# A third width, 144 columns, for the gate and up products of experts with 129 to 144 rows

## The chip, the core and the metric

The kernel runs on one core of a Trainium2 chip. The metric is the device time of one execution in microseconds; a lower number is better. The kernel before takes 750.63 us, the median of three runs.

## What is computed

One layer of an encoder over 768 tokens of width 1024. After a mixing part (projection, a recurrent group, a spatial gating group, an output projection) comes the part that the change touches, a mixture of 16 experts. A router picks two experts for each token, and each expert is a gated product with an inner width of 512:

```python
for e in range(N_EXPERTS):
    hdn = jax.nn.silu(t @ w1[e]) * (t @ w3[e])      # gate and up
    out = out + gate[:, e:e + 1] * (hdn @ w2[e])    # down
```

The reference does this for all tokens; `gate` is zero for the tokens that did not choose expert e. A per-layer embedding part and a last norm follow. All of it is float32.

## The kernel before, in words

**Rounds.** The expert part is a chain of 16 rounds, one for each expert, r = 0 to 15. A round works on the rows of the tokens that chose its expert, gathered ahead by GpSimd into `moe["xg", par]` (the first 128 rows) and `moe["xg2", par]` (up to 32 more, `CAP` is 160). `par` is r modulo 2; even rounds read the transposed rows from `regT`, odd ones from `regN`, so these names in the trace tell the two apart. Rows over 160 would go to further rounds at the end; the register `more` counts these.

**One round on TensorE** (`one_round`, L990): it reads the number of rows of its expert and of the next one from `table` into registers (L992, L994). Then come two halves. Each half computes two of the four blocks of 128 inner columns, gate and up, with `hidden` (L955): two blocks times two weights times 8 steps over the width of 1024, 32 float32 matmuls, whose moving operand has `n` columns, one for each row of the expert. Behind the first half stand four transposes of the next expert's rows (L933), behind the second half four more. Then the down products, 24 matmuls in two parts (L964 to L966), between which the further 32 rows of the next expert are turned if it has over 128 (L935), and at last, if the round's own expert has over 128 rows, 16 matmuls for those further rows (L973, L976).

**The width.** The 32 matmuls of a half are in the program once for each width of `CLASSES` (L52), and `by_size` (L979) puts them behind branches on the register: it splits the list of widths in two, asks whether the count fits the lower part, and goes down until one width is left. With the two widths 128 and 160 that is one branch ahead of each half, and a jump over the 160 body for those that ran the 128 body. The seven pairs of rounds from 2 to 15 are one loop, `pe.Fori(1, NE // 2)` at L1064, whose body is an even and an odd round; rounds 0 and 1 are written out ahead of it (L1062, L1063). Behind the loop stands a branch over the code for rows above 160 (L1068), then the products of the embedding part (L875).

**Others.** ScalarE (silu, copies) and VectorE (products with up, the low parts of numbers) read from PSUM at the full 160 columns in every round, whatever the width was (L1289, L1783). SyncE loads three weights of 2 MB for each round into slots of `ring`, each as soon as TensorE has done with what lay there (L507, L510).

Of the kernel before, what the change touches and what calls it, by code (L numbers as in the profile page):

```python
# [48 lines left out]
MAX_OVER = 2 * NTOK // CAP  # L49
NROUND = NE + MAX_OVER  # L50
NSLOT = NROUND * CAP
CLASSES = (128, 160)  # L52
NYG = 4
MASKED = -3.0e38

# [5 lines left out]
def hybrid_encoder_kernel(nc, x_prompt, x_sample, p_prompt, p_sample, g_mix, w_in, conv_w, conv_b, lru_w_a,  # L61
# [11 lines left out]
    with ExitStack() as ctx:  # L73
# [277 lines left out]
        class Chain:  # L351
# [5 lines left out]
            def post(self, ins):  # L357

                self.n += 1
                ins.then_inc(self.sem, 1)  # L360
# [350 lines left out]
        def _(pe):  # L711
# [266 lines left out]

            def by_size(count, body, sizes=CLASSES):  # L979

                if len(sizes) == 1:
                    body(sizes[0])
                    return
                low = sizes[:len(sizes) // 2]
                with pe.If(count < low[-1] + 1):
                    by_size(count, body, low)
                with pe.Else():
                    by_size(count, body, sizes[len(low):])
# [456 lines left out]
        def _(dve):  # L1445
# [275 lines left out]
            for b in range(4):  # L1721
                post(V.memset(bank[b][:, :].rearrange("p (f s) -> p f s", f=2)[:, :, CLASSES[0]:CAP], 0.0))
            post(V.memset(bank[5][0:CAP2, 4 * NE:], 0.0))
# [211 lines left out]
```

## Time and profile before

| what | us |
|---|---|
| median of 3 runs (750.43 to 753.56) | 750.63 |
| the profiled execution | 751.04 |
| its span, first to last instruction | 749.3 |
| TensorE busy with matmuls | 722.1 |
| mean granted TensorE clock | 0.992 of full |
| rounds 0 to 15 (first gate product to last down product) | 288.5 to 652.9 |

The profile tells one execution. PE are the matmuls and PEld the weight loads of TensorE; a row on PEldq is TensorE's sequencer, which reads the program, takes the branches and hands the matmuls on. A float32 matmul of the program gives two PE and two PEld records, so a half of a round shows as 64 matmuls.

### The profile page before, as it was taken

To read this page: it belongs to the slowest core of one execution; us is meant where nothing else is said; L and a number is where in the kernel's file an instruction comes from. 1 tells how busy PE (TensorE), PEld (TensorE's weight loads), DVE (VectorE), ACT (ScalarE), POOL (GpSimd) and SP (SyncE) were. 2 spreads that over 40 slices of the span, in tenths; PEclk is the share of its full clock that TensorE was granted. 3 is DMA by queue.
4 is the path that set the end of the run, shared out by engine and by line. 5 is a ranking of instruction groups with operands and counts; after the bars stand their busy time and mean duration, and the time that the engine had idled before them with its cause. 6 is when DMAs were issued, how large, how long until landed. Compare 5 with 4: busy or idle time off the path is not lost.

```text
span 749.3 us, 12071 instructions
## 1 busy us (share of the span) xinstructions
PE 722.1 (96%) x4424; PEld 624.1 (83%) x4425; DVE 420.6 (56%) x729; ACT 323.3 (43%) x593; POOL 136.8 (18%) x170
## 2 busy tenths in 40 slices
PE   6999999999999988999999999999999999899996
PEld 4987777787888857989988988999999999848885
DVE  5867986894654488424442342445455444567664
ACT  6508659673502135324441332344344433484243
POOL 5465104151001003000000000000000000043420
PEclk9999999999999999999999999999999999999998
DMA  9909924402225177978996595799999999363212
GB/s 312 285 1 328 270 55 154 169 1 105 92 88 193 57 280 247 313 270 307 367 360 242 215 363 200 288 338 343 364 346 337 330 336 361 139 205 113 98 43 85
DMA packets 78162, 168.59 MB, mean 225 GB/s; under 512 B 7581, under 2 KB 19305, under 8 KB 78122
## 3 DMA queue, kind: packets, MB, share of 16 engines
q1 hardware_dynamic: 70128, 141.53, 53.5%
q0 software_dynamic: 4448, 14.62, 6.3%
q10 hardware_dynamic: 3546, 11.91, 4.1%
q8 instruction: 26, 0.43, 0.2%
q14 instruction: 14, 0.11, 0.0%
HBM read 143.99 MB, written 24.05 MB: 224 GB/s over the span
## 4 chain that ended last, share of the span: by engine, by line
PE 92%; DVE 3%; ACT 2%; issue 1%; POOL 0%; ACTq 0%; DMA 0%; POOLq 0%; DVEq 0%
PE bank L743 35%; PE bank L955 32%; PE bank L731 5%; PE bank L964 4%; PE bank L966 4%; PE bank L965 4%; PE bank L723 2%; PE bank L933 2%; ACT ring_r L1377 1%; PE bank L976 1%; PE bank L973 1%; PE bank L875 1%; PE bank L715 1%; DVE regN L1458 0%; PE bank L935 0%
## 5 line engine op out<-in xcount | busy, mean ns | idle before, releaser
L743 PE MATMUL bank<-ring_r,regT_r 128*128 128x512 f32 (+1 forms) x648 | 161.5, 384 | 3.3 <-DVE regT_r L1571 1.7
L743 PEld LDWEIGHTS bank<-ring_r,regT_r 128*128 128x128 f32 x648 | 117.9, 188 | 28.7 <-issue 3.4
L955 PE MATMUL bank<-regT,ring 128*128 128x128 f32 (+1 forms) x1024 | 123.7, 282 | 2.9 <-issue 1.9
L955 PEld LDWEIGHTS bank<-regT,ring 128*128 128x128 f32 x1024 | 121.7, 191 | 5.3 <-issue 5.1
L955 PE MATMUL bank<-regN,ring 128*128 128x128 f32 (+1 forms) x1024 | 123.2, 281 | 0.1
L955 PEld LDWEIGHTS bank<-regN,ring 128*128 128x128 f32 x1024 | 122.1, 191 | 1.1 <-issue 0.5
L643 POOL DMA_INDIRECT regT<-n_scratch,idsi x17 | 16.1, 950 | 307.8 <-PEq L922 178.2
L743 PE MATMUL bank<-regT_r,ring_r 128*128 128x256 f32 (+1 forms) x256 | 66.1, 347 | 1.8 <-POOL ring_r L608 1.8
L1783 DVE TENSOR_TENSOR regR<-regR,bank 128x256 f32<-128x256 f32 x32 | 13.5, 421 | 89.2 <-ACT regR L1289 88.9
L1289 ACT ACTIVATE regR<-bank 128x320 f32<-128x320 f32 x32 | 13.8, 431 | 92.6 <-PE bank L955 92.6
L743 PEld LDWEIGHTS bank<-regT_r,ring_r 128*128 128x128 f32 x256 | 46.2, 199 | 7.2 <-DVE h_r L1464 2.0
L1132 ACT ACTIVATE regN<-h 128x1024 f32<-128x1024 f32 x23 | 24.3, 1061 | 60.9 <-DVE h L1592 40.8
L965 PE MATMUL bank<-ring_r,regR_r 128*128 128x512 f32 x128 | 49.9, 390 | 0.0
L438 POOL TENSOR_TENSOR ring_r<-ring,ring_r 128x1024 fp32r<-128x1024 f32 x16 | 41.4, 2621 | 27.3 <-ACT ring_r L430 27.3
L743 PE MATMUL bank<-h_r,ring_r 128*128 128x512 f32 (+1 forms) x128 | 44.3, 346 | 0.0
L596 POOL TENSOR_SCALAR small<-small 128x1 f32<-128x1 f32 (+1 forms) x26 | 10.1, 389 | 167.3 <-ACT regN L1132 100.7
L1795 DVE TENSOR_TENSOR ring_r<-ring,wsT_r 128x512 fp32r<-128x512 f32 x32 | 20.7, 688 | 29.8 <-ACT wsT_r L1304 29.8
L743 PE MATMUL bank<-ring_r,h_r 128*128 128x512 f32 x96 | 37.4, 389 | 0.0
L1801 DVE COPY regN<-bank 128x512 f32<-128x512 f32 x16 | 11.1, 691 | 45.8 <-PE bank L966 45.8
L1304 ACT ACTIVATE wsT_r<-ring 128x512 fp32r<-128x512 f32 x32 | 18.4, 622 | 33.1 <-issue 24.8
L1311 ACT ACTIVATE regN<-bank 128x512 f32<-128x512 f32 x16 | 9.6, 597 | 48.5 <-PE bank L966 48.5
L743 PE MATMUL bank<-ring_r 128*128 128x512 f32 x96 | 30.3, 396 | 0.0
(319 smaller groups left out, 1240.0 us busy)
## 6 DMA issues: line engine op xcount, KB each, us to landing
ring<-in_w_exp_down SPq DMA_DIRECT2D x16, 2048.0 KB, 15.9
ring<-in_w_exp_gate SPq DMA_DIRECT2D x16, 2048.0 KB, 9.4
ring<-in_w_exp_up SPq DMA_DIRECT2D x16, 2048.0 KB, 16.6
ring<-in_w_in SPq DMA_DIRECT2D x3, 2048.0 KB, 11.7
y_scratch<-zeros SPq DMA_DIRECT2D x4, 1408.0 KB, 12.9
y_scratch<-regN ACTq DMA_DIRECT2D x11, 384.0 KB
h<-in_x_sample SPq DMA_DIRECT2D x8, 512.0 KB, 10.0
y_scratch<-zeros SPq DMA_DIRECT2D x4, 1024.0 KB, 11.0
```

The lines of the kernel that those rows point to most:

```text
L438: engine.tensor_tensor(ringR[:, lo, c], ring[:, lo, c], ringR[:, hi, c].bitcast(F32), ALU.subtract).then_inc(lo_ready[unit], 1)
L643: nc.gpsimd.indirect_dma_start(moe["xg", par][0:n, :], None, n2_dram, bass.IndirectOffsetOnAxis(ap=ids[0:n, :], axis=0)).then_inc(gathered ...
L723: q = nc.tensor.transpose(ps(name)[:src.shape[1], at:at + n], src, ident[0:n, 0:n])
L731: q = nc.tensor.matmul(out, a, b, start=(k == 0), stop=(k == len(pairs) - 1))
L743: q = nc.tensor.matmul(out, a, b, start=(n == 0), stop=(n == len(passes) - 1))
L955: q = nc.tensor.matmul(bank[b][:, col:col + n], slot3(s)[:, k, f * P:(f + 1) * P], moe["xT", par][:, k, 0:n], start=(k == 0), stop=(k == K ...
L964: nc.tensor.matmul(out[:, :], x_high, high, start=(f == 0), stop=False)
L965: nc.tensor.matmul(out[:, :], x_high, low, start=False, stop=False)
L966: q = nc.tensor.matmul(out[:, :], x_low, high, start=False, stop=(f == F4 - 1))
L1132: nc.scalar.activation(ntok[:, i, :], h[:, i, :], ACT.Square, accum_out=dst).then_inc(done, 1)
L1304: nc.scalar.activation(down_hi[f][j], down_part(par, f, j), ACT.Copy).then_inc(down_high_done, 1)
L1795: V.tensor_tensor(down_low(par, f, j), down_part(par, f, j), down_hi[f][j].bitcast(F32), ALU.subtract).then_inc(down_low_done, 1)
```

## The change

`CLASSES` gets a third width. For each half `by_size` now writes three bodies: for at most 128 rows as before, for 129 to 144 rows one of 144 columns, for more one of 160. The list is split into (128) and (144, 160), so a second branch stands ahead of the two wider bodies, and none is added on the way to the 128 body.

```diff
-CLASSES = (128, 160)
+CLASSES = (128, 144, 160)
```

What that adds to TensorE's program, on the piece of the difference for the first half of round 0, the first of ten such places (two halves in each of rounds 0 and 1, of the two rounds of the loop, and of the round for rows above 160):

```order
@@ -649,4 +649,7 @@
 L955 MATMUL bank<-regT,ring 128x128 x32
 L985 UNCONDITIONAL_BRANCH
+L985 COMPARE_AND_BRANCH
+L955 MATMUL bank<-regT,ring 128x144 x32
+L985 UNCONDITIONAL_BRANCH
 L955 MATMUL bank<-regT,ring 128x160 x32
 L987 UNCONDITIONAL_BRANCH
```

The 144 body stands between the other two, with a branch ahead of it and a jump behind it. The other engines' programs are the same as before.

The head of the loop and the first half of its even round, on TensorE, before:

```order
L1064 ISA
L992 TENSOR_LOAD table
L992 ISA x2
L994 ISA
L994 TENSOR_LOAD table
L994 ISA x2
L997 ISA
L998 ISA
L1002 ISA
L985 COMPARE_AND_BRANCH
L955 MATMUL bank<-regT,ring 128x128 x32
L985 UNCONDITIONAL_BRANCH
```

and the same place from the branch on in the changed program:

```order
L985 COMPARE_AND_BRANCH
L955 MATMUL bank<-regT,ring 128x128 x32
L985 UNCONDITIONAL_BRANCH
L985 COMPARE_AND_BRANCH
L955 MATMUL bank<-regT,ring 128x144 x32
L985 UNCONDITIONAL_BRANCH
L955 MATMUL bank<-regT,ring 128x160 x32
L987 UNCONDITIONAL_BRANCH
```

The loop holds four such places, so its body is longer by 4 times 32 matmuls and their branches. A round with at most 128 rows now jumps over two bodies where it jumped over one.

## Rows read from the trace of the kernel before

**Rows 1.** The page: TensorE's busy time, and the chain that ended last by line.

```profile
PE 722.1 (96%) x4424; PEld 624.1 (83%) x4425; DVE 420.6 (56%) x729; ACT 323.3 (43%) x593; POOL 136.8 (18%) x170
...
PE bank L743 35%; PE bank L955 32%; PE bank L731 5%; PE bank L964 4%; PE bank L966 4%; PE bank L965 4%; PE bank L723 2%; PE bank L933 2%; ACT ring_r L1377 1%; PE bank L976 1%; PE bank L973 1%; PE bank L875 1%; PE bank L715 1%; DVE regN L1458 0%; PE bank L935 0%
```

**Rows 2.** Waits of TensorE, 285 to 660 us: total us, times, longest.

```profile
PE bank L955 <- issue: 1.9, 5, 0.9
```

**Rows 3.** Waits of SyncE's queue, 240 to 660 us, same columns.

```profile
SPq L510 <- PE bank L955: 211.5, 14, 18.2
```

**Rows 4.** Groups by line and shape: busy us, mean ns, idle before.

```profile
L955 PE MATMUL bank<-regN,ring 128*128 128x160 f32 x256 | 35.5, 299 | 0.1
L955 PE MATMUL bank<-regT,ring 128*128 128x160 f32 x256 | 35.5, 299 | 0.9 <-issue 0.9
```

**Rows 5.** Timeline of PE, rounds 0 and 1: start, us, line, tiles, count.

```profile
296.18 7.31 PE L955 MATMUL bank<-regT,ring 128*128 128x128 f32 x64
303.33 0.60 PE L933 MATMUL bank<-ident,regT 128*128 128x128 f32 x4
...
309.88 0.39 PE L966 MATMUL bank<-regR_r 128*128 128x512 f32 x1
310.33 8.96 PE L955 MATMUL bank<-regN,ring 128*128 128x160 f32 x64
...
319.57 8.86 PE L955 MATMUL bank<-regN,ring 128*128 128x160 f32 x64
328.26 0.60 PE L933 MATMUL bank<-ident,regT 128*128 128x128 f32 x4
```

**Rows 6.** Timeline of PE where the loop turns, rounds 3 to 4 and 7 to 8.

```profile
379.73 0.39 PE L966 MATMUL bank<-regR_r 128*128 128x512 f32 x1
381.05 8.96 PE L955 MATMUL bank<-regT,ring 128*128 128x160 f32 x64 [0.93 <-issue]
...
486.16 7.40 PE L955 MATMUL bank<-regT,ring 128*128 128x128 f32 x64 [0.25 <-issue]
```

**Rows 7.** Branches of `by_size`, whole run: ns min/median/max, first and last start.

```profile
L985 PEldq COMPARE_BRANCH  x56: 67/169/436, 288.4 to 644.9; - x56
```

**Rows 8.** The same line, 309 to 311 us and then 435 to 437 us.

```profile
L985 PEldq COMPARE_BRANCH  x1: 322/322/322, 310.0 to 310.0; - x1
...
L985 PEldq COMPARE_BRANCH  x1: 212/212/212, 435.9 to 435.9; - x1
```

**Rows 9.** Timeline of PE where the loop turns behind round 5.

```profile
437.44 0.39 PE L973 MATMUL bank<-regR_r 128*64 128x512 f32 x1
437.67 0.57 PE L955 MATMUL bank<-regT,ring 128*128 128x160 f32 x3
```

**Rows 10.** The loop's closing branch, whole run.

```profile
L1064 PEldq COMPARE_BRANCH  x7: 67/209/218, 378.5 to 650.8; - x7
```

**Rows 11.** Instruction packets by DMA queue, whole run: packets, MB, share.

```profile
q8 instruction: 26, 0.43, 0.2%
```

**Rows 12.** The same queue from 0 to 337 us.

```profile
q8 instruction: 16, 0.26, 0.3%
```

**Rows 13.** The same queue from 337 to 376 us.

```profile
q8 instruction: 5, 0.08, 0.9%
```

**Rows 14.** The same queue from 652 to 750 us.

```profile
q8 instruction: 5, 0.08, 0.3%
```

**Rows 15.** The branch over the code for rows above 160.

```profile
L1068 PEldq COMPARE_BRANCH  x1: 3317/3317/3317, 651.5 to 651.5; - x1
```

**Rows 16.** Timeline of PE behind the loop.

```profile
652.51 0.39 PE L966 MATMUL bank<-regR_r 128*128 128x512 f32 x1
655.02 12.26 PE L875 MATMUL bank<-ring,regX 128*128 128x512 f32 x24 [2.12 <-issue]
```

**Rows 17.** Busy time by stretch: PE, PEld, DVE, ACT, POOL, PEclk, DMA, GB/s.

```profile
655.00:657.70 2.70, 2.68 (x4) 1.31 (x5) 0.68 (x1) 0.00 (x0) 0.00 (x0) 0.58 0.44 124
278.00:285.00 7.00, 6.17 (x32) 2.75 (x32) 6.09 (x33) 0.79 (x2) 3.23 (x3) 0.76 0.59 202
```

**Rows 18.** Timeline of PE: eight matmuls of L875 at full clock, then across a dip.

```profile
270.32 3.67 PE L875 MATMUL bank<-ring,regX 128*128 128x512 f32 x8 [0.79 <-issue]
...
279.37 5.40 PE L875 MATMUL bank<-ring,regX 128*128 128x512 f32 x8
```

## The prediction

> **What bounds the kernel now.** I read the page first [rows 1]: TensorE is busy for 722 of 749 us, and the chain that ended last runs through its matmuls, 32% of the span through line 955, the products that the change narrows. Next the waits inside the expert part [rows 2]: ahead of line 955 TensorE stands still for 1.9 us in all 16 rounds, and for nothing but its own issue. SyncE's queue is the one that waits, 211.5 us for TensorE to give a slot of weights back [rows 3], so the weights come early. A microsecond less, or more, on TensorE between 288 and 653 us is therefore a microsecond of the end. The third thing to read is how TensorE gets its program, which the change makes longer: branches and instruction packets [rows 7 to 16].
>
> **Which rounds change.** The trace has 256 records of 160 columns on regN and as many on regT [rows 4]; a round has 128, so two odd and two even rounds have over 128 rows. By their places they are rounds 1, 4, 5 and 6. How many rows each has no view tells; worked out from the reference's inputs, experts 1, 4, 5 and 6 get 136, 133, 153 and 146. Rounds 1 and 4 take the new width, 5 and 6 stay at 160.
>
> **What the narrower products save.** From the start of a half's first product to the start of the transposes behind it a half takes 303.33 - 296.18 = 7.15 us at 128 columns and 328.26 - 319.57 = 8.69 us at 160 [rows 5]. Half way between them are 7.92 us, a saving of 0.77 us a half and, for four halves, 3.1 us. If time went purely by columns a half would be 8.69 x 144/160 = 7.82 us and the saving 3.5 us; if it moved in steps of 32 columns the saving would be nothing. I take 3.1, since 7.15 to 8.69 is already nearly the ratio of the columns. ScalarE and VectorE read 160 columns as before, and wait for TensorE, so they lose nothing.
>
> **What the branches cost.** A branch of by_size takes 67 to 436 ns, 169 in the median [rows 7]. In half 1 it is hidden: the five waits on issue [rows 2] all stand ahead of a half 0, and a second branch is hidden there too, under products and transposes still queued. In half 0 of round 1 the branch of 322 ns [rows 8] ends in the 0.22 us by which the first product comes late (310.33 against 309.88 + 0.23) [rows 5], and round 4 starts 0.93 us late [rows 6]. One more branch is paid at these two places, 0.1 us each: 0.2 us.
>
> **What the longer program costs.** This is the large term. In straight code instruction packets of 16 KB come all the way, 16 of them up to 337 us [rows 12]. While the loop is gone through for the first time, 337 to 376 us, there are 5 more [rows 13]. Behind it there are 5 [rows 14], and the whole run has 26 [rows 11]: 16 + 5 + 5. So in the 276 us in which the loop turns six more times, not one packet is fetched; TensorE keeps the whole loop. Counted from the order of the program, with four instructions for a float32 matmul, the loop has about 1,350 instructions of a program of about 7,150. With 26 packets for that program a packet holds some 270, and the loop is 5 packets long. It covers parts of six, and the one ahead of the last is fetched too: at least seven are kept. The change adds four bodies of 128 instructions and their branches, some 530. The loop then is about 1,880 long, 7 packets, covers parts of eight or nine, and with the one ahead nine or ten must be kept.
>
> The trace has the price of such a branch once. The one at line 1068 jumps over code that was never fetched and takes 3.3 us [rows 15], while a closing branch of the loop takes 0.21 us [rows 10]: 3.1 us more. Behind line 1068 TensorE has run dry for 2.12 us [rows 16], with a few products queued as cover. At the loop's turns there is less cover. It turns six times:
>
> - Behind rounds 3, 7, 9, 11 and 13, whose successor already starts 0.25 to 0.93 us late [rows 6], nothing is left to hide under: 5 x 3.1 = 15.5 us.
> - Behind round 5 the branch of the next round is done at 436.1 us [rows 8] and the queue holds work until 437.67 [rows 9], so 1.5 us are hidden and 1.6 us are paid.
> - The clock: twice TensorE stood still for about 2.1 us, ahead of 278.6 and of 655.02, and twice the granted clock then fell, to 0.76 and 0.58 in the mean of these stretches [rows 17], that is partly to the lower of its two levels, 1.2 GHz. Eight matmuls of line 875 took 5.40 us across such a dip and 3.67 us without [rows 18], 1.7 us more. After gaps of 3.3 us and more I expect it at each of the five turns, 8.5 us; bounds 0 and 8.5.
> - The first pass: rounds of at most 128 rows jump over 260 instructions at once, about a packet, where only one is fetched ahead. This may stall between 0 and 8 us over rounds 0 to 3; the five packets of 39 us [rows 13] become seven. I take 1.
>
> **The sum.** Against the profiled execution: 751.0 - 3.1 + 0.2 + 15.5 + 1.6 + 8.5 + 1 = 774.7 us. That execution lies 0.4 us above the median of 750.63, so the forecast is 774.3 us. This case's own range is 765 (no dip of the clock) to 781 (each fetch a microsecond longer, since in the loop it shares the DMA engines with the weights).
>
> **A rule on the other side of the rows.** The closing branch jumps back over five packets in 0.21 us, and no packet follows it [rows 10 to 14]. The same section of the Trainium skill also says that a taken branch whose target lies outside a window of two pages fetches that page. If this held for TensorE, the loop before would already pay at every turn, the misses would stand in both kernels, and the sum would be 751.0 - 3.1 + 0.2 - 0.4 = 747.7 us in place of 774.3. The rows contradict it, and I give it no chance.
>
> **The rivals.**
>
> - *The loop still fits.* TensorE keeps nine or more packets, and only the saving is left: 751.0 - 3.1 + 0.2 - 0.4 = 747.7 us, with the bounds of the saving 747 to 750.8. For it: the loop turns six times without one fetch. Against it: nothing seen has needed more than seven. This is the case on the other side, slightly faster; it decides at the size of the store, at or above the loop's span plus one.
> - *It fits, but the first pass stalls.* Up to 8 us on rounds 0 to 3 from jumps that run past the packet fetched ahead: 750 to 756 us. For it: the jumps get twice as long while fetches stay one ahead. Against: before, no round of the first pass is longer than the later ones of its width.
> - *The loop is fetched anew at each turn.* If a miss at the head discards what is kept, all packets come again in each of six passes, and the jumps over 260 instructions run past them: 1 to 4 us more in each of seven passes, or 780 to 800 us. For it: line 1068 shows that a jump outside what is kept restarts the fetching, with two packets within 5 us behind 652. Against: products queued ahead cover part of each stall, at line 1068 about 1.2 us (3.3 less the 2.12 run dry).
> - *The change does nothing here.* If no expert had 129 to 144 rows, only length would be added. The counts of 133 and 136 are far from both ends, so I give it no share.
>
> **How the numbers follow.** Loop head missed at each turn: 0.45, my forecast. Fetched anew with further stalls: 0.27. Still fits, saving alone: 0.20. Fits, with stalls in the first pass: 0.08. A difference of 0.5%, 3.75 us, is about what a measurement of this kernel can tell from no change. Faster than 746.9 us needs more than the largest saving, 0.03. Between 746.9 and 754.4 lie nearly all of "still fits" and half of the stalls in the first pass, 0.23. Slower than 754.4 us is the rest, 0.74. The range runs from 748, which takes in most of the case where the loop fits, to 795, which leaves out the end of the worst one.
>
> **What would show it.** Right if the profile after has: products of 144 columns in rounds 1 and 4, halves of about 7.9 us; far more than the 26 to 31 instruction packets that a longer program alone would need, at least one or two for each turn, between 380 and 660 us; closing branches at line 1064 of about 3 us in place of 0.21; idle time put down to issue ahead of each even round's first product; and dips of the clock behind it. One fetch of the head per turn means the forecast; seven or eight packets per turn mean the third rival. It is wrong if no instruction packet falls in the later passes of the loop and the closing branch still takes 0.2 us. Then the time must be near 748, and the store is larger than I took it to be.

## The result, and the profile after

The changed kernel takes 841.76 us in the median of four executions (825.98 to 854.03), the kernel before 750.53 us in the same sessions: 91 us more. The ratio is 1.105, with a 95% interval of 1.100 to 1.110; it is made from the two shorter executions, 825.98 and 835.67 us, while the profile below is of the longest, 854.03 us. The forecast of 774 us was right in its direction and in the part of the chip, and far off in size: 24 us slower were forecast, 91 were measured, and the range ended at 795.

The page of the profile after, against [rows 1] and [rows 11]:

```profile
span 852.3 us, 12083 instructions
PE 750.0 (88%) x4424; PEld 647.7 (76%) x4425; DVE 420.7 (49%) x729; ACT 324.4 (38%) x593; POOL 137.6 (16%) x170
PEclk9999999999999799999789899798897988999998
q8 instruction: 84, 1.38, 0.7%
PE 84%; issue 10%; DVE 3%; ACT 3%; ACTq 0%; POOL 0%; DMA 0%; POOLq 0%; DVEq 0%
```

The number of matmuls is the same and every other engine is as busy as before. Three things are new: 84 instruction packets where there were 26, 10% of the chain put down to issue, and a granted clock that falls again and again from the 14th of 40 slices on.

The waits of TensorE between 285 and 760 us (total, times, longest), against [rows 2]:

```profile
PE bank L955 <- issue: 57.3, 16, 9.0
PE bank L933 <- issue: 14.7, 7, 3.6
```

Before, these were 1.9 us and none. So 70 us are time in which TensorE had no instruction to run, either ahead of a half or ahead of the transposes behind it. The matmuls themselves take 750.0 - 722.1 = 27.9 us more, though fewer columns pass: that is the clock. Over the loop the mean granted clock (the column PEclk, the third from the right) is 0.91, where it was 1.00. After, then before:

```profile
345.00:752.00 407.00, 339.10 (x2307) 311.56 (x2305) 136.52 (x279) 122.78 (x265) 21.52 (x24) 0.91 0.68 244
...
337.60:652.90 315.30, 313.38 (x2314) 291.60 (x2312) 136.40 (x281) 121.78 (x265) 21.58 (x24) 1.00 0.85 310
```

70 + 28 and a wait ahead of line 944 that is 1.6 us longer than before make 100 of the 103 us between the two profiled executions.

The branches (count, ns min/median/max), against [rows 10], [rows 7] and [rows 15]:

```profile
L1064 PEldq COMPARE_BRANCH  x7: 67/6878/7333, 397.4 to 752.9; - x7
...
L985 PEldq COMPARE_BRANCH  x68: 68/234/6785, 288.6 to 746.3; - x68
...
L1068 PEldq COMPARE_BRANCH  x1: 3463/3463/3463, 753.8 to 753.8; - x1
```

The closing branch takes 6.1 to 7.3 us each time it is taken (the seventh time, 67 ns, the loop ends), not 0.2 and not the 3.3 I had. Its first start, 397.4 us, is 18.9 us later than before [rows 10]: that much is lost ahead of the first turn, and some 83 us in the six turns and the passes behind them. The jumps of by_size stall too, up to 6.8 us. And the packets by stretch, 0 to 345 us, 345 to 397 us (first pass of the loop), 397 to 753 us (six more passes), against [rows 12 to 14]:

```profile
q8 instruction: 18, 0.29, 0.3%
...
q8 instruction: 7, 0.11, 0.9%
...
q8 instruction: 54, 0.88, 1.0%
```

54 packets in six passes are nine a pass: the whole loop is fetched anew each time.

The narrower products do what they should. Round 4, second half, takes 427.12 - 419.28 = 7.84 us, where a half of 160 columns took 8.69 [rows 5]:

```profile
419.28 8.01 PE L955 MATMUL bank<-regT,ring 128*128 128x144 f32 x64
427.12 0.60 PE L933 MATMUL bank<-ident,regT 128*128 128x128 f32 x4
```

### The profile page after: what moved, and what is told of

The parts are those of the page before. It is cut to its first block, busy times and chain, and to the rows that moved or that the text cites. A ratio compares the mean times of both kernels' runs of the same rounds, so it can differ in the third digit from the quotient of the medians.

```text
span 852.3 us, 12083 instructions
## 1 busy us (share of the span) xinstructions
PE 750.0 (88%) x4424; PEld 647.7 (76%) x4425; DVE 420.7 (49%) x729; ACT 324.4 (38%) x593; POOL 137.6 (16%) x170
## 4 chain that ended last, share of the span: by engine, by line
PE 84%; issue 10%; DVE 3%; ACT 3%; ACTq 0%; POOL 0%; DMA 0%; POOLq 0%; DVEq 0%
PE bank L743 31%; PE bank L955 30%; PE bank L731 4%; PE bank L964 4%; PE bank L966 4%; PE bank L965 4%; PE bank L723 2%; PE bank L933 2%; ACT ring_r L1377 1%; PE bank L976 1%; PE bank L973 1%; PE bank L715 0%; PE bank L875 0%; DVE regN L1458 0%; PE bank L935 0%
## 5 line engine op out<-in xcount | busy, mean ns | idle before, releaser
L955 PE MATMUL bank<-regT,ring 128*128 128x128 f32 (+2 forms) x1024 | 142.5, 307 | 50.8 <-issue 48.8
L955 PEld LDWEIGHTS bank<-regT,ring 128*128 128x128 f32 x1024 | 139.3, 217 | 55.5 <-issue 55.3
L955 PE MATMUL bank<-regN,ring 128*128 128x128 f32 (+2 forms) x1024 | 126.9, 286 | 8.6 <-issue 8.6
L955 PEld LDWEIGHTS bank<-regN,ring 128*128 128x128 f32 x1024 | 124.7, 197 | 11.0 <-issue 10.8
L965 PE MATMUL bank<-ring_r,regR_r 128*128 128x512 f32 x128 | 51.9, 405 | 0.0
L933 PE MATMUL bank<-ident,regT 128*128 128x128 f32 x128 | 20.3, 284 | 14.7 <-issue 14.7
```

The source lines that it names most:

```text
L933: q = nc.tensor.transpose(bank[4][:, a * P:(a + 1) * P], moe["xg", par][:, k * P:(k + 1) * P], ident[:])
L955: q = nc.tensor.matmul(bank[b][:, col:col + n], slot3(s)[:, k, f * P:(f + 1) * P], moe["xT", par][:, k, 0:n], start=(k == 0), stop=(k == K ...
L965: nc.tensor.matmul(out[:, :], x_high, low, start=False, stop=False)
```

## The experiments

The instruction counts of the loop below are good to some 50 instructions; between two kernels they differ by some 130 for each body of a half. A packet is taken at 256 instructions: e8 has 32 bodies of some 130 more than e9 and fetches 17 packets more, some 245 to a packet. The times of the kernel before in these sessions had medians of 751.4 to 753.2 us; each ratio is against it.

### e1: the same length, no narrower product

```diff
-CLASSES = (128, 144, 160)
+CLASSES = (128, 160, 160)
```

> The widths are (128, 160, 160): as much code as in the change, but no product gets narrower; it does all of the reference's work. Theory A, the length of TensorE's program costs the time: as slow as the change and 3 us more, 830 to 860 us, some 84 instruction packets, closing branches of the loop of 6 to 7 us. Theory B, the 144-column products themselves do it (slower on TensorE, or something that reads them): 750 to 752 us.

Measured: 841.05 us, ratio 1.118 (1.114 to 1.123), 70 packets, closing branches of 6.4 us in the median. The loss is in the length of the program. The 144-column products have no part in it.

The 70 packets are unevenly spread. Two of the six passes behind the first fetch two packets, as my forecast had it for all of them, the other four nine. The passes from 524 and from 575 us:

```profile
q8 instruction: 2, 0.03, 0.3%
...
q8 instruction: 9, 0.15, 1.1%
```

From closing branch to closing branch the two passes with two packets take 57.9 and 50.9 us, 8 and 9 us more than the same rounds before; the last three, with nine, take 52.9 to 56.4 us, 11 to 15 us more. So the miss at the head, with its dip of the clock, is the larger part of what a pass loses, and the other seven packets the smaller.

### e2, e3, e4: how long the loop may get

```diff
 # e2: three widths in rounds 0 and 1 only
-by_size(count, body)
+by_size(count, body, CLASSES if isinstance(r, int) else (128, 160))
 # e3: and in the even round of the loop
+... if isinstance(r, int) or (turn_next and par == 0) else (128, 160)
 # e4: and in the first half of the odd round
+... if isinstance(r, int) or (turn_next and (par == 0 or half == 0)) else (128, 160)
```

> Three widths in rounds 0 and 1 alone, which stand ahead of the loop; the loop is as before. Theory A1, the loop no longer fits what TensorE keeps: no packets from 385 us on, closing branches of 0.2 us, round 1 saves 1.55 us; with no stall of the first pass 749.0 us. Theory A2, the longer forward jumps stall wherever they run past the packet fetched ahead, loop or not: stalls of 1 to 5 us in rounds 0 and 1, 752 to 758 us.

> Three widths in rounds 0 and 1 and in the even round of the loop, two widths in its odd round: the loop has about 1,610 instructions where before it had 1,345 and the change has 1,873. Rounds 1 and 4 get the narrower products. If TensorE keeps eight packets of 256 instructions: the loop from 18.5 to 24.8 packets into the program, with the one ahead, covers exactly eight, so no packets in its later passes and 747 to 752 us, by what the first pass stalls. If it keeps seven: as the change, packets in every pass, above 790 us.

> As the one before, and the first half of the loop's odd round gets three widths too: 1,741 instructions, ending 25.3 packets into the program. If TensorE keeps eight packets: one too many with the one ahead, so packets in every pass and closing branches of 6 to 7 us, 800 to 850 us. If it keeps nine or more: no packets in the later passes, 747 to 755 us. If the cost grew with length step by step rather than at an edge: half way between the one before and the change.

| kernel | instructions in the loop | packets from 390 us to its end | us | ratio |
|---|---|---|---|---|
| e2 | about 1,350, as before | 0 | 758.84 | 1.008 (1.005 to 1.011) |
| e3 | about 1,610 | 0 | 763.00 | 1.014 (1.012 to 1.017) |
| e4 | about 1,740 | 45 | 824.80 | 1.097 (1.092 to 1.101) |
| the change | about 1,870 | 54 | 841.76 | 1.105 (1.100 to 1.110) |

The closing branches of e3 and of e4:

```profile
L1064 PEldq COMPARE_BRANCH  x7: 67/209/218, 392.2 to 662.9; - x7
```

```profile
L1064 PEldq COMPARE_BRANCH  x7: 67/7467/7726, 387.9 to 723.5; - x7
```

Some 130 instructions more, and 62 us more: an edge, not a slope. It is not a clean one. At one of its six turns, 460.9 us, the closing branch of e4 takes 0.21 us, and no packet comes in the pass behind it; the other five passes fetch nine each. So once, TensorE had the whole loop of 1,740 instructions in its store, and why not at the other turns these runs do not tell.

e2 shows the second cost by itself. Its loop turns freely, but it is 6 to 7 us slower than before, and the waits on issue ahead of line 955 are 8.0 us where they were 1.9. 6.3 of them lie in rounds 0 and 1, where code comes for the first time, three bodies to a half. e3 has no packet in its later passes, as expected for a store of eight, but at 763.00 us it is 11 us above the 747 to 752 expected: I had no price for these stalls.

### e5: the same loop, at another place in the program

```diff
+never = pe.value_load(table[0:1, T_NUM:T_NUM + 1], min_val=0, max_val=MAX_OVER)
+with pe.If(never > 3):
+    for k in range(20):
+        nc.tensor.matmul(...)
 with pe.Fori(1, NE // 2) as i:
```

> The kernel of e3 (763 us) with 80 instructions (20 matmuls) and a few more ahead of the loop, behind a branch that never enters them: the loop is exactly as long as in e3 and only begins 0.35 of a packet later in the program, from 18.85 to 25.1 packets. If eight packets on a fixed grid are kept, the loop now covers eight and the one ahead makes nine: packets in every pass, closing branches of 6 to 7 us, 805 to 830 us. If what counts is the loop's length alone (any grid), it fits as in e3: 760 to 768 us.

The added code is never entered. Measured: 755.56 us, ratio 1.004 (1.001 to 1.007), no packet between 390 and 655 us. The expectation from a fixed grid of packets was wrong: the loop of 1,610 instructions is kept at either place. Why it is even 7 us faster than e3 isn't settled; its waits on issue ahead of line 955 come out smaller, 7.8 us against 10.7.

### e6: the change with lighter loads

This kernel leaves out seven eighths of the gate and up weights in the loop, so experts 2 to 15 are computed with other weights; its waits and matmuls are those of the change.

```diff
-sp.dma_start(dst, w.rearrange("(k p) n -> p k n", p=P)).then_inc(ring_in[s], 16)
+part = slice(0, dst.shape[1] if isinstance(e, int) or src is w_exp_down else 1)
+sp.dma_start(dst[:, part, :], w.rearrange("(k p) n -> p k n", p=P)[:, part, :]).then_inc(ring_in[s], 16)
```

> The changed kernel, but in the loop the gate and up weights are loaded for one eighth only (the rest of each slot keeps the numbers of earlier experts), so experts 2 to 15 are computed with wrong weights and the loads of the loop fall from 6 to 2.5 MB a round. All waits and all matmuls stay. Theory C, an instruction packet is late because it shares the DMA engines with the weights: closing branches fall from 6 to 7 us toward the 3.3 us of line 1068, the other stalls shrink too, 785 to 810 us. Theory D, the fetch takes that long by itself: closing branches stay at 6 to 7 us, 825 to 850 us.

Measured: 793.08 us, ratio 1.053 (1.046 to 1.061). The closing branch (its line is one further down here):

```profile
L1065 PEldq COMPARE_BRANCH  x7: 67/3557/3887, 385.8 to 691.6; - x7
```

3.6 us in place of 6.9, nearly what line 1068 takes before, when the DMA engines have little to do. The trace tells where the difference lies. In the change the packet that a closing branch waits for starts 3.5 to 4.7 us after the branch and then takes 1.0 to 1.2 us; in e6 it starts 1.0 to 1.4 us after it and takes 1.1 to 1.5; at line 1068 before, 1.0 and 1.0. A packet's own transfer is as short beside the weights as without them, and it is its start that is late. More than half of the loss goes away with less than half of the loads. Not all of that is the price of a miss, for packets fell as well, to 49: in five of the six turns only two came, the head's and one more, and in one turn nine. Why a pass fetches two at one time and nine at another stays open.

### e7 and e13: a hint for the closing branch

```diff
-with pe.Fori(1, NE // 2) as i:
+with nc.Fori(1, NE // 2, engines=[mybir.EngineType.PE], hint_back_edge=True) as i:
```

e13 has that too, and for the loop's rounds `CLASSES = (128, 144, 152, 160)`.

> The changed kernel with a prefetch hint for the loop's closing branch at the top of each iteration. If the hint brings the head's packet in and it stays: closing branches of 0.2 us, 6 x 6.5 us and some dips of the clock saved, 785 to 805 us, the forward jumps still stall. If the packet is overwritten before the loop turns, or the hint is without effect: 825 to 850 us.

> As e7 (766 us, hint for the closing branch), with a fourth width of 152 columns in the loop's rounds: the loop has about 2,405 instructions, 9.4 packets, where e7 has 1,878, 7.3 packets. If TensorE keeps eight packets and it was only the packet fetched ahead that was one too many in the change: the hint cannot help here, packets in every pass, above 840 us. If it keeps many more and the change only lost its place at the turn: as e7, no packets in the later passes, 760 to 775 us.

Measured: e7 takes 766.11 us, ratio 1.018 (1.010 to 1.026), some 75 us less than the change from one instruction in the loop, and far below the 785 to 805 expected, which took off the closing branches alone. e13 takes 878.68 us, ratio 1.168 (1.163 to 1.173). Closing branches and packets of e7, then of e13:

```profile
L1064 PEldq COMPARE_BRANCH  x7: 76/228/233, 392.6 to 664.1; - x7
...
q8 instruction: 30, 0.49, 0.3%
```

```profile
L1064 PEldq COMPARE_BRANCH  x7: 76/3337/4082, 402.3 to 778.3; - x7
...
q8 instruction: 93, 1.52, 0.7%
```

With the hint no packet is fetched in the six later passes of e7. So TensorE can keep the change's whole loop of some 1,870 instructions, 7.3 packets, where without the hint it did not, and did not reliably keep 1,740. What is one too many is then, I take it, the packet fetched ahead beyond the loop's end, and the hint points that fetch at the loop's head, which is there. The packets up to the first closing branch bear this out, in the change, 0 to 397 us, and in e7, 0 to 392.5 us:

```profile
q8 instruction: 25, 0.41, 0.4%
...
q8 instruction: 24, 0.39, 0.4%
```

One fewer is fetched with the hint. It is an inference all the same, and not all runs fit it: e4 kept its loop at one turn, and e5 was kept where the reckoning of its expectation had one packet too many. At some 2,400 instructions, 9.4 packets, the loop is not kept even with the hint; there is no run of that length without it. The edge lies between 7.3 and 9.4 packets of loop with the hint, and between 6.3 and 6.8 without it. The Trainium skill, "Runtime: NRT & Kernel Launch", section "Instruction fetch mechanics", gives 2,048 instructions, eight packets, for TensorE. e3, e4, e7 and e13 agree with it, if the packet ahead counts; e5 does not on the grid that its expectation assumed.

### e8 and e9: no loop

```diff
-with pe.Fori(1, NE // 2) as i:
+for i in range(1, NE // 2):
```

e8 with three widths, e9 with two.

> Three widths, and the loop's seven passes written out, so there is no backward branch; all code is new each time. If the backward branch costs the most (6 to 7 us each): 41 us and its dips of the clock less than the change, 780 to 800 us, with the forward jumps stalling in every round as they do in rounds 0 to 3 of the change. If fetching code at this pace is itself the bound (three bodies to a half, one taken): near the change, 815 to 850 us.

> Two widths, and the loop's seven passes written out: all code is fetched, in every round, but only two bodies to a half, so 0.5 packet less per half than in e8 (797 us, three widths written out). If it is the length of code per half that makes the jumps stall: hardly a stall, 749 to 753 us, since the first pass of the kernel before had none; the turns of the loop save their 0.25 us each. If code that is new each time stalls at any pace: 765 to 790 us.

Measured: e8 797.14 us, ratio 1.059 (1.053 to 1.065), 73 packets. e9 748.96 us, ratio 0.997 (0.995 to 1.000), 56 packets. Waits of TensorE, 285 to 760 us, in e8, then in e9:

```profile
PE bank L955 <- issue: 19.0, 9, 4.6
PE bank L933 <- issue: 16.5, 7, 3.5
```

```profile
PE bank L955 <- issue: 1.2, 2, 1.0
```

Code that is new all the time costs nothing with two bodies to a half, and 48 us with three, one of which is run. So the forward jumps are a cost of their own. A half of 7 to 8 us runs through 1.0 packet of program before and 1.5 after, and a packet that a branch waits for takes several microseconds to come. That the jumps outrun a fetch that is only one packet ahead fits these numbers; no run changes how far ahead is fetched.

### e10, e11 and e12: what can be had

```diff
 # e10: two widths; (144, 160) in round 1, (128, 160) elsewhere
+by_size(count, body, (144, 160) if isinstance(r, int) and r == 1 else (128, 160))
 # e12: the loop written out as in e9, and
+by_size(count, body, (144, 160) if isinstance(r, int) and r in (1, 4) else (128, 160))
 # e11: kernel before; marked at the start of each odd round of the loop
+exit_loc.append(pe.mark_branch_hint_location())
 ...
-with pe.If(more > 0):
+pe.br_lt(more, 1, on_true=after_rest, on_false=rest).branch_hint(exit_loc[0])
+with nc.body(rest, valid_engines=[mybir.EngineType.PE]):
```

> No third body anywhere: in round 1 alone the two widths are 144 and 160 instead of 128 and 160 (right for any input; with under 129 rows that round would only be slower). The program is as long as before. Round 1's two halves take 7.84 us in place of 8.69: 1.7 us less than before, 0.2%, so a ratio of 0.998. If the 144-column products gave nothing on the path, 1.000.

> The kernel before (two widths) with a prefetch hint, given at the start of each odd round of the loop, for the branch behind the loop that jumps over the code for rows above 160. That branch took 3.3 us, TensorE ran dry for 2.1 us and lost some 1.7 us to the clock. If a hint fetches the target while the loop still runs and it is kept: the branch takes 0.2 us, 2 to 4 us less than before, a ratio of 0.995 to 0.997. If the hinted packet pushes out one of the loop's: stalls at each turn, 790 us or more. If the hint is lost because other branches are taken in between: no difference.

> The loop written out as in e9, two bodies to a half everywhere, and rounds 1 and 4 with the widths (144, 160) in place of (128, 160): both narrower rounds and no third body. Right for any input, but rounds 1 and 4 are chosen for this routing. From e9's 748.96: less 1.7 us for round 4 and 1.7 us for round 1, 745.6 us, a ratio of 0.993. If the narrower rounds make code come late, as much as e9, 749 us.

e10: 748.90 us, ratio 0.997 (0.996 to 0.999): faster, by what was expected within the interval. Its round 1 has halves of 7.85 us (325.66 - 317.81):

```profile
317.81 8.01 PE L955 MATMUL bank<-regN,ring 128*128 128x144 f32 x64
325.66 0.60 PE L933 MATMUL bank<-ident,regT 128*128 128x128 f32 x4
```

e11: the branch takes 0.35 us instead of 3.3, and TensorE no longer runs dry behind the loop. The time is the same, ratio 1.001 (0.999 to 1.003). The branch, and TensorE's only wait from 650 to 670 us:

```profile
L1073 PEldq COMPARE_BRANCH  x1: 351/351/351, 651.1 to 651.1; - x1
...
PE bank L723 <- DVE h L1865: 3.9, 1, 3.9
```

TensorE is earlier there and then waits for VectorE, which adds up the experts' rows, so that stall was hidden.

e12: 744.52 us, ratio 0.991 (0.988 to 0.993), the fastest of all: faster than before and than the change. Both narrow rounds, no third body, no loop. It took 4.4 us off e9 where 3.4 were expected. It is right for any routing, but rounds 1 and 4 are chosen for this one.

### e14 and e15: the hint with light loads

> e7 with the light loads of e6 (gate and up of experts 2 to 15 loaded for one eighth, so their products are computed with wrong weights). What is left of e7's loss, 14 us, is stalls of jumps in the first pass. Theory C, packets come late because the weights fill the DMA engines: these stalls shrink, against e15 a loss of 2 to 6 us. Theory D, they take that long by themselves: 12 to 16 us above e15.

> The kernel before with the light loads of e6 and e14, same wrong weights in experts 2 to 15: the measure for these two. TensorE never waited for a weight, so 747 to 751 us; if the loads slowed anything else on the path, less.

e15 takes 750.58 us, ratio 0.998 (0.996 to 1.000): the weights' loads alone cost the kernel before nothing. e14 takes 760.08 us, 9.5 us above it; e7 is 13 us above its own measure. The waits on issue ahead of the halves and transposes fall from 13.4 us in e7 to 8.9. So these stalls shrink with the loads by about a third. The loss lies between theory C's 2 to 6 us and theory D's 12 to 16: the price of a packet at a jump depends on the loads in part only.

## Why the prediction was wrong

**Which rounds, and the saving.** Right. Rounds 1 and 4 ran at 144 columns, a half in 7.84 us; I had taken 7.92 and given 7.82 as the bound by columns. The saving is 3.4 us, not 3.1.

**The branches.** A small term that didn't show: round 1 starts 0.21 us late with the added branch and 0.22 without it.

**That the loop would outgrow what TensorE keeps.** Right, and the step that carried the direction. "At least seven are kept ... with the one ahead nine or ten must be kept": the edge is between 6.3 and 6.8 packets of loop, and the hint takes it away from the change (e3, e4, e7). How the store goes about it isn't settled by this, as e4 and e5 show.

**"Then ... its closing branch must wait for a packet".** This is the step that failed, as the likeliest case had it: one miss at each turn and the rest kept. In fact the loop was fetched whole in each pass, nine packets of it. That was the third rival, with a chance of 0.27; but its 780 to 800 us did not reach the measured time either, since its "1 to 4 us more" a pass came on top of the same low price for the head.

**The price of a miss.** 3.1 us, from the one branch of line 1068 [rows 15], measured 5.9 to 7.1: the closing branch takes 6.1 to 7.3 us in place of 0.2. That branch is taken when the weights are all loaded, and in the loop the DMA engines are busy for 0.85 of the time. I had named this as a microsecond at most. e6 gives the closing branch 3.6 us once the loads are cut. Six turns cost 41 us of sequencer time instead of 19. This weighs more than the number of packets. I had 25.6 us for six turns, stalls and clock, 4.3 each. The two passes of e1 that went as I forecast lost 8 and 9 us; six like them would be 51 us, an estimate, and the change lost 83.

**The forward jumps.** "I take 1", with 8 as the bound, over rounds 0 to 3. The change is 18.9 us behind at its first closing branch, though round 1 is 1.7 us shorter by then. e7, whose turns cost nothing, is 14 us behind there. e2, with three bodies in rounds 0 and 1 alone, gives 6 to 7 us for these two. Since all packets are fetched again, each later pass pays too: e8, which has these jumps and no backward branch, loses 48 us against e9.

**The clock.** I had five dips of 1.7 us, 8.5 us in all; the matmuls took 27.9 us more. e1, which has as many columns as before, shows it without the saving: 751.7 - 722.1 = 29.6 us more, with 20 waits on issue ahead of lines 955 and 933, or 1.5 us a wait. So the cost of one was near, and the number far too low.

**The sum.** In the profiled execution: 70 us of stalls instead of 18, 28 us of clock instead of 8.5. The sum of 774.7 us adds up as it stands. The chances do not quite: the terms make 0.21 for about the same and 0.76 for slower, where 0.23 and 0.74 are stated. What is left open: why one pass fetches nine packets and another two or none (two in e1 and e6, none in e4), and why e5 beats e3.

## What to carry to other kernels

The program itself is a stream that the DMA engines carry (e6), and a body that is never run is still fetched and jumped over (e8 against e9). Ahead of a change that adds a variant of a large body inside a loop, count the loop's instructions on its engine against the packets in the profile: if packets stop coming after the first pass the loop is kept, and here growth by under a third cost far more than the work that it saved. If it must grow, hint the closing branch, or write the loop out and leave each round with two bodies; and take the price of a miss from a stretch where the DMA engines are as busy as in the loop.

## What the hardware showed that I had not expected

- The edge is sharp: some 1,610 instructions of loop run at 763 us and some 1,740 at 825 us; the second fetches nine packets in five of six passes and none in the other.
- A single hint at the loop's top takes a loop of some 1,870 instructions from 841.8 to 766.1 us.
- A branch that misses takes 3.3 to 4.4 us with little other DMA work (line 1068) and 5.4 to 7.7 us beside the weights (line 1064 of the change, e1 and e4). The packet's own transfer takes 1.0 to 1.2 us in the change as at line 1068 before; it starts 3.5 to 4.7 us after the branch in place of 1.0.
- Stalls of TensorE of a few microseconds cost again in the clock: 28 us on top of 70.
- The changed kernel's executions spread from 826 to 854 us, where most of the kernel before's lie within 750 to 755.
